# The gate matrix of a PEER layer: summed in HBM by GpSimd's indirect DMAs instead of multiplied out of one-hot matrices

## Chip, cores and metric

The kernel runs on one core of a Trainium2 chip. The metric is the device time of one execution in microseconds, here the median of three runs.

## What is computed

Two transformer-like blocks on 256 tokens of width 2048, in float32. The change touches only the PEER layer of the first block, a mixture of 16,384 one-row experts of which each token picks 8 x 16:

```python
scores = jnp.einsum('thpc,hpnc->thpn', q, sub_keys)          # 8 heads, 2 halves, 128 keys
vals, idx = lax.top_k(scores, 16)
cand = (vals[..., 0, :, None] + vals[..., 1, None, :]).reshape(T, 8, 256)
top_vals, top_c = lax.top_k(cand, 16)
experts = (i1 * 128 + i2).reshape(T, 128)                    # i1, i2: idx of the winners
gates = jax.nn.softmax(top_vals, axis=-1).reshape(T, 128)
hdn = jax.nn.gelu(jnp.einsum('ted,td->te', expert_down[experts], x))
y = jnp.einsum('te,ted->td', gates * hdn, expert_up[experts])
```

The kernel does not gather expert rows. It multiplies all 16,384 rows of `expert_down` and of `expert_up`, and weights the hidden values of each token by a gate matrix G[expert, token] that is zero where an expert was not picked and holds the sum of its gates where it was picked (by several heads, possibly).

## The kernel before, in words

**Units.** All weights are streamed in units of 512 KB: SP loads a unit into the ring `raw` (four slots), ACT copies it rounded into `whi` (three slots), DVE writes the remainder `wlo = raw - whi`, and PE multiplies both parts with the two parts of the activations. Every engine walks through the same list of units in program order, and the work around the matmuls is hung on unit numbers: `tick(u)` on PE, `step(u)` on DVE and ACT, the loop over `now` on SP. Unit u of `whi` can be written when PE has finished unit u-3.

**Stages around the change.** `wf` is the second half of the attention's output product (units 113 to 128), `pq` the PEER query (129 to 160), `down` the product with `expert_down` (161 to 416, two units for each of 128 groups), `up` the product with `expert_up` (417 to 672). Group i of `down` gives the hidden values of experts 128 i to 128 i + 127 for all 256 tokens. ACT copies one half of the PSUM bank to `HB` (`half`), DVE adds the other (`whole`, which frees the bank), POOL multiplies by the rows' normalization (`rows3`), and ACT applies `gelu(i)`, one group later. In `up` DVE multiplies by the gates (`weight(i)`).

**Routing.** `route(k)` runs in the first 162 units of `down`, a step a unit. On DVE: top 16 of the scores (steps 0 to 39), the candidate sums (41 to 48), top 16 of those (49 to 68), the softmax (69 to 71, the exponential on ACT), the look-up of i1 and i2 (72 to 95, one operation on 1024 elements a step), for both tiles of 128 tokens. At step 96 PE transposes i1, i2 and the gates, so that a token's 128 picks lie on the partitions. Then, in steps 97 to 161, `gate_rows(n)` on DVE makes two 128x128 matrices for each of four tokens (the one-hot rows of i2; the one-hot rows of i1 times the gate), PE multiplies them (`gate_batch`: four matmuls in float32 for each of 64 batches, each token's gates as a 128x128 matrix), ACT copies the bank to `GB` and issues a store of 1 MB for every 16 tokens (`gate_out`). The scratch `g_d` in HBM then holds the gate matrix, and SP loads it in pieces of 1 MB (`load_g`) for `weight(i)` in `up`; the gates of the first two groups come to `g0` ahead of that.

Of the kernel before, what the change touches and what calls it, by code (L numbers as in the profile page):

```python
# [8 lines left out]
F32 = mybir.dt.float32  # L9
# [126 lines left out]
def _build(nc, I, out, ctx):  # L136
# [3 lines left out]
    def alloc(stack, name, shape, dt=F32):  # L140
# [40 lines left out]
    g_d = nc.dram_tensor("gate_scratch", (16, 128, 2048), F32, kind="Internal").ap()  # L181
    g_v = g_d.rearrange("b p (m n c) -> m p b n c", m=16, c=16)
# [36 lines left out]
    g0 = alloc(E_, "g0", [128, 16, 2, 16])  # L219
    rows3 = alloc(E_, "rows3", [128, 256])  # L220

# [16 lines left out]
    GT = hb(25088, 256).rearrange("p (t h n) -> p t h n", t=2, h=8)  # L238
    GS = hb(25344, 32).rearrange("p (s t h) -> p s t h", s=2, t=2)
    JT = hb(25856, 768).rearrange("p (s c) -> p s c", s=3)  # L240
    AB = hb(26624, 2048).rearrange("p (i s c n) -> p i s c n", i=2, s=2, c=4)
    GB = hb(28672, 4096).rearrange("p (i n c) -> p i n c", i=2, c=16)
# [76 lines left out]
    JTF = [plan.side() for _ in range(2)]  # L319
    GBF = [plan.side() for _ in range(64)]  # L320
# [39 lines left out]
    ROUTE = 162  # L360
# [45 lines left out]
    def _(e):  # L406
# [9 lines left out]
        def load_g(n, a=0, z=8):  # L416
            i = n % 2
            if n >= 2:
                w.wait_ge(s_um, 8 * n - 8)
            e.dma_start(gbuf[:, i, :].rearrange("p (b n c) -> p b n c", b=16, c=16)[:, :, a:z, :].bitcast(F32),  # L420
                        g_v[n][:, :, a:z, :]).then_inc(s_gl[i], 16)
# [10 lines left out]
        for u in range(NRAW, NU + NRAW + NSPL):  # L432
# [21 lines left out]
            if now == G["down", 120].end:  # L454
                w.wait_ge(s_gw[0], 128)
                w.wait_ge(s_gw[1], 128)
                e.dma_start(g0[:, :, :, :], g_v[0][:, :, 0:2, :]).then_inc(s_g0, 16)
# [39 lines left out]
    def _(e):  # L497
# [88 lines left out]
        def route(k):  # L586
            if k == 96:
                w.wait_ge(s_rc, 40)
                b, b2 = vacant(JTF[0]), vacant(JTF[1])
                for t in range(2):  # L590
                    turn_round(b[:, t * 128:t * 128 + 128], IX[:, 0, t, :])
                for t in range(2):
                    turn_round(b[:, 256 + t * 128:384 + t * 128], IX[:, 1, t, :])
                for t in range(2):
                    tr = turn_round(b2[:, t * 128:t * 128 + 128], GT[:, t, :, :].rearrange("p h n -> p (h n)"))
                tr.then_inc(s_jt, 1)
            if 98 <= k <= 161:
                gate_batch(k - 98)

# [49 lines left out]
        def tick(u):  # L649
# [12 lines left out]
            if DOWN0 <= u < DOWN0 + ROUTE:  # L662
                route(u - DOWN0)
# [193 lines left out]
    def _(e):  # L857
# [131 lines left out]
        def top16(p, lists, val, idx, base):  # L989
            n = len(val)  # L990
            o = 8 * (p // 3)
            for i in lists:
                src, v, ix = val[i]
                before = base + p * n + i + 1 - n
                if p:
                    w.wait_ge(s_top, before)
                if p in (0, 3):
                    e.max(v[:, o:o + 8], src).then_inc(s_top, 1)
                if p in (1, 4):
                    e.max_index(ix[:, o:o + 8], v[:, o:o + 8], src).then_inc(s_top, 1)  # L1000
                if p == 2:
                    e.match_replace(src, v[:, 0:8], src, -3.0e38).then_inc(s_top, 1)

        one = [(SC[:, t, 2 * h + s, :], V16[:, t, h, s, :], I16[:, t, h, s, :]) for t in range(2) for h in range(8) for s in range(2)]
        two = [(CD[:, t, h, :], TV[:, t, h, :], TC[:, t, h, :]) for t in range(2) for h in range(8)]

        def gate_rows(n):
            i = n % 2
            for fill in JTF:
                evacuated(fill)  # L1010
            if n >= 2:
                w.wait_ge(s_gb, n - 1)
            for c in range(4):
                t = n * 4 + c
                e.tensor_scalar(AB[:, i, 0, c, :], iota, JT[:, 0, t:t + 1], None, ALU.is_equal).then_inc(s_oh, 1)  # L1015
                e.tensor_scalar(AB[:, i, 1, c, :], iota, JT[:, 1, t:t + 1], JT[:, 2, t:t + 1], ALU.is_equal, ALU.mult).then_inc(s_oh, 1)  # L1016

        def route(k):
            if k < 40:
                p, q = k // 8, k % 8  # L1020
                if k == 0:
                    for fill in SCF:
                        evacuated(fill)
                top16(p, range(4 * q, 4 * q + 4), one, None, 0)
            if k == 40:
                w.wait_ge(s_top, 160)
                e.tensor_copy(hb(22528, 512), hb(22016, 512, U32)).then_inc(s_rc, 1)
            if 41 <= k < 49:
                t, h0 = (k - 41) // 4, 2 * ((k - 41) % 4)
# [3 lines left out]
            if 49 <= k < 69:  # L1033
                p, q = (k - 49) // 4, (k - 49) % 4
                w.wait_ge(s_rc, 9)
                top16(p, range(4 * q, 4 * q + 4), two, None, 160)
            if k == 69:
                w.wait_ge(s_top, 240)
                e.tensor_scalar(hb(23552, 256, U32), hb(23296, 256, U32), 4, None, ALU.logical_shift_right).then_inc(s_rc, 1)
                e.tensor_scalar(hb(23808, 256, U32), hb(23296, 256, U32), 15, None, ALU.bitwise_and).then_inc(s_rc, 1)  # L1040
                w.wait_ge(s_rc, 11)
                e.tensor_copy(hb(24064, 512), hb(23552, 512, U32)).then_inc(s_rc, 1)
            if k == 70:
                tt(GT, TV, TV[:, :, :, 0:1].to_broadcast([128, 2, 8, 16]), ALU.subtract).then_inc(s_rc, 1)
            if k == 71:
                w.wait_ge(s_gx, 1)
                e.tensor_reduce(GS[:, 0], GT, AX, ALU.add).then_inc(s_rc, 1)
                w.wait_ge(s_rc, 14)
                e.reciprocal(GS[:, 1], GS[:, 0]).then_inc(s_rc, 1)
                w.wait_ge(s_rc, 15)  # L1050
                tt(GT, GT, GS[:, 1].unsqueeze(3).to_broadcast([128, 2, 8, 16]), ALU.mult).then_inc(s_rc, 1)
# [897 lines left out]
```

## Time and profile before

| | |
|---|---|
| median of three runs | 2939.56 us (2937.03 to 2940.48) |
| the profiled execution: its own time | 2936.61 us |
| its span, first to last instruction | 2934.8 us |
| busy share: PE, DVE, ACT, POOL | 98%, 65%, 48%, 4% |
| HBM traffic | 190 GB/s over the span |

PE is TensorE's matmuls, DVE is VectorE, ACT is ScalarE, POOL is GpSimd, SP is SyncE (it issues DMAs only). A busy share is an average over stages with different limits. Times in the rows are microseconds from the start of the span unless they are marked ns.

### The profile page before, as it was taken

Reading aid. Unit: us, or ns where it says so; the run is one execution under the profiler, and the core shown is the slowest. Engines: PE = TensorE matmul, PEld = TensorE weight load, DVE = VectorE, ACT = ScalarE, POOL = GpSimd, SP = SyncE. Lnnn points to the kernel's source line nnn. Section 1 sums busy time; section 2 is a strip of 40 time slices with the busy share of each in tenths; the row PEclk is TensorE's granted clock in tenths of the full one; section 3 lists DMA queues with packets and bytes.
Section 4 is the critical chain, followed back from the end, with each engine's and each line's share of the span. In section 5 each row is a group of like instructions: output and inputs, shape, how many; then the busy total and the mean of one; then the engine's idle time right before and its main releaser. Section 6 shows DMA issues by size and latency. Waiting matters only on the chain. (4 is left out here: it accounts for less than half of the span.)

```text
span 2934.8 us, 40340 instructions
## 1 busy us (share of the span) xinstructions
PE 2862.8 (98%) x15486; PEld 2465.3 (84%) x15486; DVE 1898.3 (65%) x3196; ACT 1413.9 (48%) x2024; POOL 103.9 (4%) x132
## 2 busy tenths in 40 slices
PE   8999999999999999999999999997999999999998
PEld 6878888888899988887888888886888888999886
DVE  5556665688999964455555555556677766555555
ACT  4444654444545544444444444445554545444454
POOL 0000000011211111110000000000000000000000
PEclk9999999999999999999999999998999999999999
DMA  7643456555556665567766776764554455555554
GB/s 253 209 147 119 137 177 223 161 188 190 189 195 216 215 208 188 190 193 220 222 213 216 226 230 221 240 207 132 186 172 145 147 159 193 187 187 187 183 195 152
DMA packets 180783, 558.94 MB, mean 190 GB/s; under 512 B 20704, under 2 KB 51696, under 8 KB 177648
## 3 DMA queue, kind: packets, MB, share of 16 engines
q1 hardware_dynamic: 177856, 538.48, 57.1%
q10 hardware_dynamic: 2736, 17.89, 1.5%
q8 instruction: 124, 2.03, 0.3%
q14 instruction: 67, 0.55, 0.1%
HBM read 535.31 MB, written 20.99 MB: 190 GB/s over the span
## 5 line engine op out<-in xcount | busy, mean ns | idle before, releaser
L871 DVE TENSOR_TENSOR wlo<-raw,whi 128x1024 fp32r<-128x1024 f32 (+1 forms) x965 | 1182.4, 1226 | 880.7 <-ACT whi L1507 876.4
L1507 ACT ACTIVATE whi<-raw 128x1024 fp32r<-128x1024 f32 (+1 forms) x965 | 1016.1, 1055 | 932.3 <-PE bank L501 916.2
L501 PE MATMUL bank<-aX,whi 128*128 128x512 f32 (+1 forms) x4000 | 1014.4, 395 | 2.5 <-ACT whi L1507 1.4
L501 PE MATMUL bank<-whi,aX 128*128 128x512 f32 x3008 | 933.9, 391 | 16.2 <-ACT whi L1507 12.2
L501 PEld LDWEIGHTS bank<-aX,whi 128*128 128x128 f32 (+1 forms) x4000 | 717.1, 188 | 136.7 <-issue 3.6
L501 PEld LDWEIGHTS bank<-whi,aX 128*128 128x128 f32 x3008 | 566.0, 188 | 135.6 <-ACT whi L1507 11.9
L501 PE MATMUL bank<-wlo,aX 128*128 128x512 f32 x1504 | 587.1, 390 | 2.0 <-DVE wlo L871 1.9
L501 PEld LDWEIGHTS bank<-aX,wlo 128*128 128x128 f32 (+1 forms) x3984 | 542.7, 190 | 40.1 <-DVE wlo L871 0.5
L501 PE MATMUL bank<-aX,wlo 128*128 128x256 f32 (+1 forms) x3984 | 557.7, 282 | 0.1
L501 PEld LDWEIGHTS bank<-wlo,aX 128*128 128x128 f32 x1504 | 283.1, 188 | 62.7 <-DVE wlo L871 4.4
L1507 ACT ACTIVATE aX<-HB 128x256 fp32r<-128x256 f32 x128 | 53.4, 418 | 214.6 <-DVE HB L874 214.6
L1493 POOL TENSOR_TENSOR HB<-HB,rows 128x256 f32<-128x256 f32 x128 | 103.7, 810 | 1220.5 <-DVE HB L874 1220.5
L1507 ACT ACTIVATE HB<-bank 128x256 f32<-128x256 f32 (+1 forms) x208 | 91.3, 439 | 111.3 <-PE bank L501 109.6
L1016 DVE TENSOR_SCALAR HB<-small,HB 128x128 f32<-128x128 f32 x256 | 100.3, 392 | 0.0
L874 DVE TENSOR_TENSOR aX<-HB,aX 128x256 fp32r<-128x256 f32 x128 | 54.4, 425 | 61.0 <-ACT aX L1507 61.0
L501 PE MATMUL bank<-HB 128*128 128x128 f32 x576 | 75.0, 275 | 3.1 <-DVE HB L874 3.1
L501 PEld LDWEIGHTS bank<-HB 128*128 128x128 f32 x576 | 69.8, 192 | 3.5 <-issue 3.2
L1015 DVE TENSOR_SCALAR HB<-small,HB 128x128 f32<-128x128 f32 x256 | 70.3, 275 | 0.0
L874 DVE TENSOR_TENSOR HB<-bank,HB 128x256 f32<-128x256 f32 x144 | 60.2, 418 | 0.8 <-ACT HB L1507 0.8
L1507 ACT ACTIVATE HB<-HB 128x256 f32<-128x256 f32 x129 | 53.1, 412 | 2.1 <-POOL HB L1493 1.9
L1507 ACT ACT_TABLE_LOAD x35 | 44.9, 1283 | 18.2 <-DVE dn L939 12.5
L874 DVE TENSOR_TENSOR HB<-HB,aX 128x256 f32<-128x256 f32 x126 | 52.8, 419 | 0.0
(208 smaller groups left out, 1740.9 us busy)
## 6 DMA issues: line engine op xcount, KB each, us to landing
raw<-in_w_down SPq DMA_DIRECT2D x256, 512.0 KB, 3.6
raw<-in_w_up SPq DMA_DIRECT2D x256, 512.0 KB, 3.9
raw<-in_w_in SPq DMA_DIRECT2D x176, 512.0 KB, 3.8
raw<-in_w_out SPq DMA_DIRECT2D x32, 512.0 KB, 3.5
raw<-in_w_pq SPq DMA_DIRECT2D x32, 512.0 KB, 3.6
gate_scratch<-HB ACTq DMA_DIRECT2D x16, 1024.0 KB, 4.8
raw<-in_w_o SPq DMA_DIRECT2D x32, 512.0 KB, 4.3
raw<-in_w_pg SPq DMA_DIRECT2D x32, 512.0 KB, 4.2
```

The costliest lines, as they stand in the source:

```text
L501: return e.matmul(o, lhsT, rhs, start=start, stop=stop, skip_group_check=True)
L871: e.tensor_tensor(wlo[:, s, 0:n], raw[:, r, 0:n], whi[:, s, 0:n].bitcast(F32), ALU.subtract).then_inc(s_lo, 1)
L874: return e.tensor_tensor(o, a, b, op)
L1015: e.tensor_scalar(AB[:, i, 0, c, :], iota, JT[:, 0, t:t + 1], None, ALU.is_equal).then_inc(s_oh, 1)
L1016: e.tensor_scalar(AB[:, i, 1, c, :], iota, JT[:, 1, t:t + 1], JT[:, 2, t:t + 1], ALU.is_equal, ALU.mult).then_inc(s_oh, 1)
L1493: e.tensor_tensor(h, h, rows3[:, :], ALU.mult).then_inc(s_hr3, 1)
L1507: return e.activation(o, i, f, **k)
```

## The change

The gate matrix is no longer multiplied out on PE.

- SP writes zeros over all 16 MB of `g_d` in 16 DMAs of 1 MB, one every third unit from unit 113 on; POOL fills the source with zeros first.
- Routing is done for token tile 0 in 49 steps and then for tile 1 in 49 steps. Its last step computes `place` = expert x 256 + token, the element of `g_d` to which a gate belongs.
- POOL issues 256 indirect DMAs (`scatter`), one for each tile, head and rank: 128 single elements of 4 bytes, each added to its place in HBM. Two heads of a token can pick the same expert, so the first of the 16 DMAs of a head waits until all DMAs of the head before it, of the same tile, have landed. The heads stand in the order (0,0) to (0,4), then in turn (0,5), (1,0), (0,6), (1,1), (0,7), (1,2), then (1,3) to (1,7).
- POOL multiplies by `rows3` only in groups 0 to 47, and issues three scatters behind each of groups 26 to 47; DVE does the multiplication from group 48 on. POOL issues the other scatters in one go, then loads `g0`, for which DVE waits at group 124. SP waits for all scatters at the start of `up`.
- Transposes, one-hot rows, matmuls, copies and stores of the gates are gone, and the scratch is laid out so that a gate load has pieces of 1 KB instead of 512 B.

```diff
+    g_d = nc.dram_tensor("gate_scratch", (128 * 128 * 256, 1), F32, kind="Internal").ap()
+    g_z = g_d.rearrange("(q n) o -> q (n o)", q=128)
+    g_v = g_d.rearrange("(i p t) o -> p i (t o)", p=128, t=256)
...
-    JTF = [plan.side() for _ in range(2)]
-    GBF = [plan.side() for _ in range(64)]
-    ROUTE = 162
+    ROUTE = 98
+    ZERO0 = G["wf", 0].first
+    OWN3 = 48
...
+            if ZERO0 <= now < ZERO0 + 48 and (now - ZERO0) % 3 == 0:
+                z = (now - ZERO0) // 3
+                w.wait_ge(s_zs, 1)
+                e.dma_start(g_z[:, z * 2048:z * 2048 + 2048], zeros).then_inc(s_zf, 16)
             if now == UP0:
                 w.wait_ge(s_mm, UP0)
+                for t in range(2):
+                    w.wait_ge(s_gs[t], 2048)
                 load_g(0, 2, 8)
                 load_g(1)
...
-        def gate_batch(n):
-            w.wait_ge(s_oh, 8 * n + 8)
-            b = vacant(GBF[n])
-            for c in range(4):
-                last = mm(b[:, c * 128:c * 128 + 128], AB[:, n % 2, 1, c, :], AB[:, n % 2, 0, c, :], True, True)
-            last.then_inc(s_gb, 1)
...
+        def route(step):
+            t, k = step // 49, step % 49
+            top, rc = 120 * t, 26 * t
...
+            if k == 48:
+                w.wait_ge(s_rc, rc + 24)
+                w.wait_ge(s_tok, 2)
+                e.scalar_tensor_tensor(IX[:, 0, t, :], IX[:, 0, t, :], 128.0, IX[:, 1, t, :], ALU.mult, ALU.add).then_inc(s_rc, 1)
+                w.wait_ge(s_rc, rc + 25)
+                e.tensor_scalar(place[:, t, :], IX[:, 0, t, :], 256.0, st[:, 22 + t:23 + t], ALU.mult, ALU.add).then_inc(s_rc, 1)
...
+            h = HB[:, i * 256:i * 256 + 256]
+            whole(G["down", i], h)
+            if i >= OWN3:
+                evacuated(G["down", i].fills[0])
+                tt(h, h, rows3[:, :], ALU.mult).then_inc(s_hr3v, 1)
...
+        def scatter(t, h, n):
+
+            if n == 0:
+                w.wait_ge(s_rc, 26 * t + 26)
+                w.wait_ge(s_zf, 256)
+                if h:
+                    w.wait_ge(s_gs[t], 256 * h)
+            c = 16 * h + n
+            e.indirect_dma_start(g_d, bass.IndirectOffsetOnAxis(ap=place[:, t, c:c + 1], axis=0), gate[:, t, c:c + 1], None,
+                                 compute_op=ALU.add).then_inc(s_gs[t], 16)
+
+        w.wait_ge(s_ht, 32)
+        e.memset(zeros, 0.0).then_inc(s_zs, 1)
+        order = [(0, h) for h in range(5)] + [(x % 2, 5 + x // 2 if x % 2 == 0 else x // 2) for x in range(6)] + [(1, h) for h in range(3, 8)]
+        todo = [(t, h, n) for t, h in order for n in range(16)]
+        at = 0
         w.wait_ge(s_free[R3F[0]], R3F[1])
-        for i in range(128):
+        for i in range(OWN3):
             b, n = G["down", i].fills[0]
             h = HB[:, i * 256:i * 256 + 256]
             w.wait_ge(s_free[b], n)
             e.tensor_tensor(h, h, rows3[:, :], ALU.mult).then_inc(s_hr3, 1)
+            if i >= 26:
+                for x in todo[at:at + 3]:
+                    scatter(*x)
+                at += 3
+        for x in todo[at:]:
+            scatter(*x)
+        for t in range(2):
+            w.wait_ge(s_gs[t], 2048)
+        e.dma_start(g0[:, :, :], g_v[:, 0:2, :]).then_inc(s_g0, 16)
```

On PE, where the gate matmuls begin (behind the units of step 96). The rows of the kernel before; `bank<-HB` of four matmuls is one batch, `bank<-small,HB` the transposes:

```order
L501 MATMUL bank<-aX,wlo 128x256 x8
L513 MATMUL bank<-small,HB 128x128 x6
L501 MATMUL bank<-aX,whi 128x512 x8
L501 MATMUL bank<-aX,wlo 128x256 x8
L501 MATMUL bank<-aX,whi 128x512 x8
L501 MATMUL bank<-aX,wlo 128x256 x8
L501 MATMUL bank<-HB 128x128 x4
L501 MATMUL bank<-aX,whi 128x512 x8
L501 MATMUL bank<-aX,wlo 128x256 x8
L501 MATMUL bank<-HB 128x128 x4
```

The same place in the changed kernel:

```order
L503 MATMUL bank<-aX,whi 128x512 x8
L503 MATMUL bank<-aX,wlo 128x256 x8
L503 MATMUL bank<-aX,whi 128x512 x8
L503 MATMUL bank<-aX,wlo 128x256 x8
L503 MATMUL bank<-aX,whi 128x512 x8
L503 MATMUL bank<-aX,wlo 128x256 x8
```

Nothing is left on PE between two units of `down`.

On POOL in the changed kernel, around groups 29 to 32 (`L1484` is the multiplication by `rows3`, `L1471` a scatter):

```order
L1484 TENSOR_TENSOR HB<-HB,rows 128x256 [waits s_free2]
L1471 DMA gate_scratch<-gate,place 4194304x1 x3
L1484 TENSOR_TENSOR HB<-HB,rows 128x256 [waits s_free3]
L1471 DMA gate_scratch<-gate,place 4194304x1 x3
L1484 TENSOR_TENSOR HB<-HB,rows 128x256 [waits s_free0]
L1471 DMA gate_scratch<-gate,place 4194304x1
L1471 DMA gate_scratch<-gate,place 4194304x1 [waits s_gs0]
L1471 DMA gate_scratch<-gate,place 4194304x1
L1484 TENSOR_TENSOR HB<-HB,rows 128x256 [waits s_free1]
```

Before, POOL had 128 such multiplications and nothing between them. The row with `s_gs0` is the first scatter of head 1, and a multiplication now stands behind it in POOL's queue.

On SP in the changed kernel, around the end of `wf` (`L457` writes zeros, `L446` stores the block's activations, `L453` loads the keys, `L415` loads units):

```order
L415 DMA raw<-in_w_pq 128x1024 [waits s_lo] x3
L457 DMA gate_scratch<-HB 128x2048
L415 DMA raw<-in_w_pq 128x1024 [waits s_lo]
L446 DMA h_scratch<-X 128x4096 [waits s_free3,s_free0,s_free2,s_free1]
L453 DMA HB<-in_keys 128x2048 [waits s_nt,s_free5,s_free6,s_free4,s_free7,s_spill]
L415 DMA raw<-in_w_pq 128x1024 [waits s_lo] x2
L457 DMA gate_scratch<-HB 128x2048
L415 DMA raw<-in_w_pq 128x1024 [waits s_lo] x3
```

Before, the rows of zeros were not there, and the 1 MB stores of the gates stood on ACT's queue in the middle of `down`.

## Rows read from the trace of the kernel before

**Rows 1.** The page: busy us of engines; its costliest group (count, busy us, mean ns)

```profile
PE 2862.8 (98%) x15486; PEld 2465.3 (84%) x15486; DVE 1898.3 (65%) x3196; ACT 1413.9 (48%) x2024; POOL 103.9 (4%) x132
...
L871 DVE TENSOR_TENSOR wlo<-raw,whi 128x1024 fp32r<-128x1024 f32 (+1 forms) x965 | 1182.4, 1226 | 880.7 <-ACT whi L1507 876.4
```

**Rows 2.** Waits of PE, the longest in total: us, times, longest us

```profile
PE bank L513 <- DVE scr L905: 17.4, 1, 17.4
```

**Rows 3.** Timeline of POOL: groups 47, 81, 102, 124, 127 of `down`

```profile
818.50 0.73 POOL L1493 TENSOR_TENSOR HB<-HB,rows 128x256 f32<-128x256 f32 x1 [4.84 <-DVE HB L874]
...
1066.95 0.74 POOL L1493 TENSOR_TENSOR HB<-HB,rows 128x256 f32<-128x256 f32 x1 [3.79 <-DVE HB L874]
...
1184.27 0.74 POOL L1493 TENSOR_TENSOR HB<-HB,rows 128x256 f32<-128x256 f32 x1 [4.85 <-DVE HB L874]
...
1307.18 0.85 POOL L1493 TENSOR_TENSOR HB<-HB,rows 128x256 f32<-128x256 f32 x1 [4.85 <-DVE HB L874]
...
1323.93 0.73 POOL L1493 TENSOR_TENSOR HB<-HB,rows 128x256 f32<-128x256 f32 x1 [4.84 <-DVE HB L874]
```

**Rows 4.** Instructions by line, 818 to 1062 us: count, busy us, mean ns

```profile
L1016 DVE TENSOR_SCALAR HB<-small,HB 128x128 f32<-128x128 f32 x256 | 100.3, 392 | 0.0
...
L1015 DVE TENSOR_SCALAR HB<-small,HB 128x128 f32<-128x128 f32 x256 | 70.3, 275 | 0.0
L501 PE MATMUL bank<-HB 128*128 128x128 f32 x512 | 67.6, 275 | 0.0
...
L1507 ACT ACTIVATE HB<-bank 128x512 f32<-128x512 f32 x64 | 38.4, 599 | 109.6 <-PE bank L501 109.6
```

**Rows 5.** Windows: us; busy of PE, PEld, DVE, ACT, POOL; clock, DMA share, GB/s

```profile
460.00:470.00 10.00, 10.00 (x62) 8.96 (x61) 5.57 (x7) 3.45 (x4) 0.00 (x0) 1.00 0.83 306
...
706.00:762.00 56.00, 56.00 (x323) 49.29 (x322) 53.64 (x130) 29.89 (x43) 9.36 (x10) 1.00 0.59 189
...
1067.00:1300.00 233.00, 233.00 (x1335) 204.96 (x1334) 115.50 (x125) 112.92 (x167) 30.98 (x42) 1.00 0.61 190
...
1400.00:1500.00 100.00, 100.00 (x443) 82.78 (x442) 59.12 (x74) 44.44 (x56) 0.00 (x0) 1.00 0.70 225
...
1980.00:2020.00 40.00, 40.00 (x178) 33.10 (x178) 23.39 (x29) 17.68 (x22) 0.00 (x0) 1.00 0.61 196
```

**Rows 6.** Timeline of a plain group of `down`: start, duration, engine

```profile
1072.54 0.74 POOL L1493 TENSOR_TENSOR HB<-HB,rows 128x256 f32<-128x256 f32 x1 [4.85 <-DVE HB L874]
...
1076.55 0.41 ACT L1507 ACTIVATE HB<-HB 128x256 f32<-128x256 f32 x1
...
1078.12 1.06 ACT L1507 ACTIVATE whi<-raw 128x1024 fp32r<-128x1024 f32 x1 [1.16 <-PE bank L501]
```

**Rows 7.** Timeline: POOL beside DVE, in `route` and in `gate_rows`

```profile
757.04 1.65 POOL L1493 TENSOR_TENSOR HB<-HB,rows 128x256 f32<-128x256 f32 x1 [3.91 <-DVE HB L874]
...
758.20 1.58 DVE L871 TENSOR_TENSOR wlo<-raw,whi 128x1024 fp32r<-128x1024 f32 x1
...
840.63 0.80 DVE L1016 TENSOR_SCALAR HB<-small,HB 128x128 f32<-128x128 f32 x1
...
841.54 0.33 DVE L1016 TENSOR_SCALAR HB<-small,HB 128x128 f32<-128x128 f32 x1
```

**Rows 8.** DMA queue of ACT, and DMA issues: KB each, us to landing

```profile
q10 hardware_dynamic: 2736, 17.89, 1.5%
...
gate_scratch<-HB ACTq DMA_DIRECT2D x16, 1024.0 KB, 4.8
...
g<-gate_scratch SPq DMA_DIRECT2D x1, 256.0 KB, 5.0
...
c_scratch<-cT SPq DMA_DIRECT2D x1, 16.0 KB, 2.6
```

**Rows 9.** Timeline and waits: what an issue takes, ACT behind the spill

```profile
852.11 0.33 ACTq L1581 DMA_DIRECT2D gate_scratch<-HB  x1
...
ACT HB L1507 <- DMA h_scratch<-X: 1.7, 1, 1.7
```

More of the change, by code:

```diff
@@ L987, in turn, with top16 @@
                     e.tensor_copy(dst[:, 2 * fp:2 * fp + 2, :].rearrange("p a c -> p (a c)"), banks[b]).then_inc(s_free[b], 1)
-        def top16(p, lists, val, idx, base):
-            n = len(val)
+        def top16(p, val, i, done):
+            src, v, ix = val[i]
             o = 8 * (p // 3)
[L992 to L1016, printed above, removed]
@@ L1018, in route @@
-        def route(k):
-            if k < 40:
-                p, q = k // 8, k % 8
+            if p:
+                w.wait_ge(s_top, done + (p - 1) * len(val) + i + 1)
+            if p in (0, 3):
+                e.max(v[:, o:o + 8], src).then_inc(s_top, 1)
+            if p in (1, 4):
+                e.max_index(ix[:, o:o + 8], v[:, o:o + 8], src).then_inc(s_top, 1)
+            if p == 2:
+                e.match_replace(src, v[:, 0:8], src, -3.0e38).then_inc(s_top, 1)
+        one = [[(SC[:, t, 2 * h + s, :], V16[:, t, h, s, :], I16[:, t, h, s, :]) for h in range(8) for s in range(2)] for t in range(2)]
@@ L1021, in route @@
+        two = [[(CD[:, t, h, :], TV[:, t, h, :], TC[:, t, h, :]) for h in range(8)] for t in range(2)]
+        def route(step):
+            t, k = step // 49, step % 49
+            top, rc = 120 * t, 26 * t
+            if k < 20:
                 if k == 0:
-                    for fill in SCF:
+                    for fill in SCF[4 * t:4 * t + 4]:
                         evacuated(fill)
[L1024 to L1027, printed above, removed]
@@ L1028, in route @@
-            if 41 <= k < 49:
-                t, h0 = (k - 41) // 4, 2 * ((k - 41) % 4)
+                for i in range(4 * (k % 4), 4 * (k % 4) + 4):
+                    top16(k // 4, one[t], i, top)
+            if k == 20:
+                w.wait_ge(s_top, top + 80)
+                e.tensor_copy(hb(22528 + 256 * t, 256), hb(22016 + 256 * t, 256, U32)).then_inc(s_rc, 1)
+            if 20 <= k < 24:
+                h0 = 2 * (k - 20)
                 o = CD[:, t, h0:h0 + 2, :].rearrange("p h (a b) -> p h a b", a=16)
@@ L1052, in route @@
[L1052 to L1054 removed]
+            if 24 <= k < 34:
+                w.wait_ge(s_rc, rc + 5)
+                for i in range(4 * (k % 2), 4 * (k % 2) + 4):
+                    top16((k - 24) // 2, two[t], i, top + 80)
+            if k == 34:
+                w.wait_ge(s_top, top + 120)
+                tc, tp = hb(23296 + 128 * t, 128, U32), hb(23552, 512, U32).rearrange("p (s t n) -> p s t n", s=2, t=2)
+                e.tensor_scalar(tp[:, 0, t, :], tc, 4, None, ALU.logical_shift_right).then_inc(s_rc, 1)
+                e.tensor_scalar(tp[:, 1, t, :], tc, 15, None, ALU.bitwise_and).then_inc(s_rc, 1)
+                w.wait_ge(s_rc, rc + 7)
+                e.tensor_copy(TF[:, :, t, :, :].rearrange("p s h n -> p s (h n)"), tp[:, :, t, :]).then_inc(s_rc, 1)
```

135 lines of the change are left out of this document (42 added, 93 removed).

## The prediction

> **What bounds the kernel now.** First the page's busy times: PE 98% of the span, DVE 65%, ACT 48%, POOL 4% [rows 1]. Then PE's waits: the longest is a single one of 17.4 us, at the seam behind `up` [rows 2]. So nearly every microsecond of matmuls is a microsecond of time, and what DVE, ACT, POOL or the DMAs do costs nothing as long as PE does not wait for it. Then the stage: POOL's multiplications follow DVE's `whole`, once a group, so their starts are a ruler for `down`. From group 102 (1184.27) to group 127 (1323.93) it is 25 groups in 139.66 us, 5.586 us a group, 2.793 us a unit. From group 47 (818.50) to group 81 (1066.95) it is 34 groups in 248.45 us [rows 3]. PE is busy all through `down` [rows 5], so that stretch is longer by PE's own extra work.
>
> **What it removes.** 34 plain groups are 34 x 5.586 = 189.9 us. The stretch with the transposes and the 64 gate batches takes 248.45, so 58.5 us go, 0.9 us a batch. The row of the gate matmuls says 67.6 us busy for 512 records [rows 4]. I take 58.5, because overlap with the units' matmuls is already out of it. On DVE 100.3 + 70.3 us of one-hot rows go, on ACT 38.4 us of copies [rows 4]; both lie beside PE and free nothing by themselves. The 16 stores of 1 MB on ACT's queue go too.
>
> **What it adds to DVE.** 80 multiplications by `rows3`. DVE is busy 115.5 of 233 us in the plain part, 2.8 us a group [rows 5], and a POOL operation of the same shape takes 0.74 us [rows 3], so even at that price a group has 3.5 of 5.59 us. Covered by half a group of idle DVE. Routing itself keeps its density: the same operations a step, in two runs of 49 steps instead of one of 96 for both tiles. In the densest part DVE is busy 53.64 of 56 us [rows 5] and PE does not wait there. The two new operations of a tile's last step are on 128 elements, about 0.3 us each by the one-hot rows' 275 ns [rows 4]. DVE may come behind by about half a microsecond once a tile. A remainder can be late by much more before PE notices: PE frees a slot three units ahead and needs the new contents two units (5.59 us) later, ACT's split takes 1.06 us [rows 6] and DVE's remainder 1.23 [rows 1]; so a split can be late by 4.5 us, a remainder by 3.3. Cost: nothing.
>
> **What it adds to the DMAs, first the zeros.** 16 MB, the same bytes as the gate stores that go, but now in front of weight loads on SP, in `wf` and `pq`. ACT's queue moved 17.89 MB in 1.5% of 2934.8 us, 44 us, so 2.6 us of the 16 engines for 1 MB [rows 8]. A unit takes about 0.6 of 2.793 us = 1.68 [rows 5, 3]. Three units and one zero DMA: 5.0 + 2.6 = 7.6 of 8.4 us, a share of 0.91. It fits on average. At the seam of `wf` and `pq` it does not: the share is 0.83 already there (460 to 470) [rows 5], ACT waits 1.7 us for the 2 MB spill [rows 9], and SP can load nothing until the spill has landed. One zero DMA in the same rings puts the landing off by 2.6 us, another follows two units later. A split can be late by 4.5 us, as above. From nothing to about 8 us (spill and keys each behind a whole zero DMA of 2.6, and the 1.7 that is waited for today: 6.9, and one more for what collides besides); I take 3 us.
>
> **What it adds to POOL: 256 scatters.** The trace has no indirect DMA and none that POOL issues. Let c be the time for which one holds POOL's queue. From below: a DMA issue on ACT's queue takes 0.33 us [rows 9]. From above: the smallest store to HBM takes 2.6 us from issue to landing [rows 8], and an issue should not hold the queue longer than a whole small DMA. The ends are far apart and nothing is near to either: software must compute 128 addresses, which is more than an issue and less than a round trip. I take the middle, 1.47 us. Three things hang on c.
>
> (1) Groups 26 to 47, three scatters behind each multiplication. POOL needs 3c + 0.81 a group (0.81 is POOL's 103.9 us over 128) [rows 1] and has 5.586. At 1.47 that is 5.2: it keeps up; it falls behind above c = 1.59. Queued behind is the next multiplication, for that ACT's `gelu`, behind that ACT's split, behind that PE. The slack of the chain: `gelu` starts 3.3 us after POOL's end (1073.28 to 1076.55), ACT then idles 1.16 us, and the split has 4.5 us [rows 6], together 9 us. Four times in these 22 groups a head must wait for the one before it, a landing of some 2.6 us [rows 8]. Each alone is inside the 9 us. If POOL never catches up between them, the loss is L1 = 22 (3c - 4.78) + 4 x 2.6 - 9.
>
> (2) The other 190, back to back, from 819 us on. DVE needs `g0` at group 124, which came at 1307.2 [rows 3] and comes 58.5 us earlier: at 1248.7, a budget of 429 us. Needed: 190 c, seven landings in the open (2.6 each; the alternating heads hide the rest) and the load of `g0`, 5.0 us [rows 8]. L2 = 190 c + 23 - 429. At 1.47 it is 302: done more than 120 us early. Late above c = 2.14.
>
> (3) DMA time. An element of 4 bytes is a packet. With gate loads of 512-byte pieces the share is 0.70 at 225 GB/s, without them 0.61 at 196 [rows 5]: in 100 us, 144 engine-us for 2.9 MB or 5700 packets, 25 ns each. Twice that for an add, which must also read: 8 packets an engine make 0.4 us a scatter, a share of 0.27 at c = 1.47, on top of 0.61. It fits.
>
> All three are nothing at the value taken. The Trainium skill, page "DMA: Bandwidth & Descriptors", section "Latency and other measured facts", gives about 1 us until the first byte of a DMA whose descriptors GpSimd writes, and calls it the emission overhead; by that c would be 1.0 and the sum the same. No row here shows it.
>
> **The sum.** The profiled execution: 2936.6 - 58.5 + 3 = 2881.1 us. The median of the runs stands 3.0 us above that execution, so 2884 us.
>
> **Rivals.**
>
> A. POOL is a little too slow, c from 1.6 to 2.2: PE is paced by POOL in groups 26 to 47. For it: DVE and POOL hold each other up. A multiplication that meets DVE's operation on two SBUF inputs took 1.65 us instead of 0.74, and DVE's own then took 1.58 instead of 1.23 [rows 1, 7]; a 128-element operation of DVE took 0.80 instead of 0.33 beside POOL [rows 7]. A scatter must read its places from SBUF. DVE's such operations fill 2.9 of 5.6 us a group, so a read waits 0.52 x 0.61 = 0.3 us on average: c = 1.8, L1 = 15 us, 2899 us. At c = 2.0 it is 28 us, 2912 us. The Trainium skill, page "SBUF — State Buffer", section "Who interferes with whom", says that a DVE instruction with two SBUF inputs contends with a GpSimd instruction that reads SBUF. By that rule, the trace agrees with 1.65 beside 0.74 us. Against it: the slack of 9 us, and a scatter's read is small. Chance 0.2.
>
> B. The other side, one mechanism: POOL's queue is held for more than 2.2 us a scatter, because the queue waits out most of each DMA. There L1 + L2 = 42 + 12 us eat the gain. At 2.4: 55 + 50, 2989 us; at 2.6: 68 + 88, about 3040 us. For it: the add needs a read and a write, and the smallest store lands after 2.6 us [rows 8]. Against it: issues on the other queues hold them 0.33 us for a transfer that lands after 4.8 [rows 8, 9]; an issue does not wait for a landing there. Chance 0.21.
>
> C. The DMA rings fill: an added element costs the engine 100 ns instead of 50, four times a packet of 512 bytes, as its read and its write follow each other. 0.8 us a scatter at c = 1.47 is a share of 0.54, with the weights 1.15, over 280 us: up to 42 us lost, 2884 to 2926 us. Against it: 25 ns a packet in the only stretch that tells. Chance 0.06.
>
> D. The change gives almost nothing because losses of A and C just cancel the 58 us: within 6 us of 2939.6. Chance 0.05.
>
> **The numbers.** My forecast, POOL keeps up and the zeros cost 0 to 8 us, has 0.48 and its own range is 2876 to 2895. A 0.2, B 0.21, C 0.06, D 0.05. What a measurement of this kernel can tell from no change is 0.2%, 6 us. Faster: the forecast, A and C, 0.74 less a little of A's upper end, 0.72. Same: 0.06. Slower: B and the rest, 0.22. The range must leave out no more than 2 in 10: from 2873 (the whole 58.5 us, and a seam that gets shorter) to 2965, which takes in the forecast, A, C, D and the near end of B.
>
> **What would show it.** Right: `down` at 5.59 us a group from group 48 to 127; scatters on POOL at 1 to 1.6 us; `g0` loaded near 1120 us; PE idle in `wf` and `pq` by at most a few us more. Wrong: in groups 26 to 47 ACT waits for POOL and a group takes more than 5.6 us (A); DVE waits at group 124 for `g0`, and SP behind it at the start of `up` (B); ACT's splits wait for `raw` while scatters run (C); or ACT and PE wait around 450 to 540 us for the zeros by more than 8 us.

## The result, and the profile after

The changed kernel takes **3001.34 us** (median of four runs, 2995.3 to 3003.97) against 2939.97 us (four runs, 2937.03 to 2940.48): ratio 1.0209, 95% interval 1.0196 to 1.0222. It is 61 us slower. The forecast was 2884 us, and the range ended at 2965.

From the page of the changed kernel, the rows that answer to [rows 1], and two groups of POOL (`L1471` is a scatter, `L1484` the multiplication by `rows3`; count, busy us, mean ns, idle us before them):

```profile
PE 2824.2 (94%) x14968; PEld 2420.9 (81%) x14968; DVE 1808.4 (60%) x2777; ACT 1381.6 (46%) x1963; POOL 591.5 (20%) x310
...
L1471 POOL DMA_INDIRECT gate_scratch<-gate,place x256 | 547.2, 2137 | 101.6 <-issue 76.5
...
L1484 POOL TENSOR_TENSOR HB<-HB,rows 128x256 f32<-128x256 f32 x48 | 53.2, 1107 | 319.5 <-DVE HB L853 319.5
```

Its waits (us in total, times, longest):

```profile
ACT HB L1507 <- POOL HB L1484: 92.0, 20, 7.1
...
DVE HB L853 <- DMA g<-gate_scratch: 86.2, 1, 86.2
...
PE bank L503 <- DVE wlo L850: 83.3, 5, 81.2
...
POOL gate_scratch L1471 <- DMA gate_scratch<-gate,place: 25.1, 10, 3.6
```

PE now waits 81.2 us in one piece for a `wlo` of DVE. DVE had not made it because it stood 86.2 us for the load of `g0`. And ACT waited 20 times for POOL's multiplication. Both kinds of wait were named in the prediction, as what would show it wrong.

To see where the time went I use the start of DVE's `whole` in groups 24, 52, 124, 125 and 127 of `down` as a ruler. Before:

```profile
689.51 0.42 DVE L874 TENSOR_TENSOR HB<-bank,HB 128x256 f32<-128x256 f32 x1
...
854.85 0.42 DVE L874 TENSOR_TENSOR HB<-bank,HB 128x256 f32<-128x256 f32 x1
...
1306.68 0.42 DVE L874 TENSOR_TENSOR HB<-bank,HB 128x256 f32<-128x256 f32 x1
...
1323.43 0.42 DVE L874 TENSOR_TENSOR HB<-bank,HB 128x256 f32<-128x256 f32 x1
```

After (here group 125 too, the second row from the end):

```profile
692.37 0.42 DVE L853 TENSOR_TENSOR HB<-bank,HB 128x256 f32<-128x256 f32 x1
...
886.64 0.42 DVE L853 TENSOR_TENSOR HB<-bank,HB 128x256 f32<-128x256 f32 x1
...
1288.88 0.42 DVE L853 TENSOR_TENSOR HB<-bank,HB 128x256 f32<-128x256 f32 x1
...
1378.94 0.42 DVE L853 TENSOR_TENSOR HB<-bank,HB 128x256 f32<-128x256 f32 x1
...
1388.79 0.42 DVE L853 TENSOR_TENSOR HB<-bank,HB 128x256 f32<-128x256 f32 x1
```

| stretch | worked out | us |
|---|---|---|
| up to group 24 | 692.37 - 689.51 | +2.9 |
| groups 24 to 52, against 28 plain ones | 886.64 - 692.37 - 28 x 5.587 | +37.8 |
| groups 52 to 124, against 72 plain ones | 1288.88 - 886.64 - 72 x 5.587 | 0.0 |
| groups 124 to 127, against before | (1388.79 - 1288.88) - (1323.43 - 1306.68) | +83.2 |
| the gate matrices, gone | [rows 3] | -58.5 |

The sum is +65.4, which is 1388.79 - 1323.43. The spans differ by 67.2 (3002.0 and 2934.8). The other 1.8 come behind group 127: by a `wlo` of `up` that starts at 1423.92 instead of 1357.13 the difference is 66.8, after a stretch in which PE's granted clock fell to half once more (last section). So what was to be removed was removed, 58.5 us, and two waits gave back 121.

**How a scatter meets `wlo`.** The timeline of DVE and POOL in the changed kernel's plain part (start, duration, then what ended the idle time before it):

```profile
977.68 1.23 DVE L850 TENSOR_TENSOR wlo<-raw,whi 128x1024 fp32r<-128x1024 f32 x1 [0.78 <-ACT whi L1507]
977.84 2.49 POOL L1471 DMA_INDIRECT gate_scratch<-gate,place  x1 [0.31 <-issue]
980.47 1.22 DVE L850 TENSOR_TENSOR wlo<-raw,whi 128x1024 fp32r<-128x1024 f32 x1 [1.56 <-ACT whi L1507]
980.64 2.48 POOL L1471 DMA_INDIRECT gate_scratch<-gate,place  x1 [0.30 <-issue]
...
983.27 1.23 DVE L850 TENSOR_TENSOR wlo<-raw,whi 128x1024 fp32r<-128x1024 f32 x1 [0.77 <-ACT whi L1507]
983.43 2.49 POOL L1471 DMA_INDIRECT gate_scratch<-gate,place  x1 [0.30 <-issue]
```

A scatter starts every 2.79 us, exactly one a unit, and each 0.16 us after a `wlo` has begun. The same queue while DVE stands:

```profile
1290.70 1.55 POOL L1471 DMA_INDIRECT gate_scratch<-gate,place  x1 [0.30 <-issue]
1292.56 1.55 POOL L1471 DMA_INDIRECT gate_scratch<-gate,place  x1 [0.30 <-issue]
...
1369.41 1.55 POOL L1471 DMA_INDIRECT gate_scratch<-gate,place  x1 [0.30 <-issue]
1372.95 0.78 POOL L1493 DMA_DIRECT2D g<-gate_scratch  x1 [1.98 <-DMA gate_scratch<-gate,place]
```

Now 1.55 us and a gap of 0.30, 1.86 a scatter. And three scatters that meet DVE in other ways, in the routing:

```profile
730.50 2.11 POOL L1471 DMA_INDIRECT gate_scratch<-gate,place  x1 [0.31 <-issue]
...
745.62 0.28 DVE L977 FIND_INDEX8 HB<-HB 128x8 uint32<-128x128 f32 x1
745.75 1.56 POOL L1471 DMA_INDIRECT gate_scratch<-gate,place  x1 [1.62 <-DMA gate_scratch<-gate,place]
```

The one at 730.50 began in the middle of a `wlo` that ran from 729.96 to 731.19, and ended at 732.61, 1.42 us behind it. The one at 977.84 ended 1.42 us behind its `wlo` too (980.33 against 978.91). All 256 scatters of the changed kernel, sorted by the DVE operation in which they started:

- 182 started inside a `wlo`. 179 of them end 1.42 to 1.47 us behind that `wlo`, whenever they began; the other three began in its last 0.04 us and last 1.56 us.
- 67 started with DVE idle: 1.55 us in the middle of their number.
- 5 started in an operation with one SBUF input (`FIND_INDEX8`, `MATCH_REPLACE8`, or a `whole`, whose other input is in PSUM): four last 1.56 us, and the first scatter of the run 1.75.
- 2 started in DVE's own multiplication by `rows3`, again two SBUF inputs: they last 1.77 us and end 1.43 behind it.

I read this so: a scatter reads SBUF in its first 0.13 us (1.55 less 1.42); the read waits for the end of a DVE operation with two SBUF inputs; then come 1.42 us of its own.

From this follows the lock. Behind a delayed scatter the next one starts 1.42 + 0.30 = 1.72 us after the end of `wlo`. The next `wlo` starts 2.79 - 1.23 = 1.56 us after that end. So the next scatter begins 0.16 us inside it and is delayed again, and so on as long as DVE runs at this pace.

The Trainium skill, page "SBUF — State Buffer", section "Who interferes with whom", says that a DVE instruction with two SBUF inputs contends with a GpSimd instruction that reads SBUF, and that a DMA which seems stalled by DVE is one whose descriptors GpSimd writes. By that rule the trace agrees: 2.49 us in `wlo`, 1.56 in operations with one input.

### The profile page after: what moved, and what is told of

It is laid out like the page before. It is cut to its first block and busy times, and to the rows that moved or that the text cites. A ratio compares the mean times of both kernels' runs of the same rounds, so it can differ in the third digit from the quotient of the medians.

```text
span 3002.0 us, 38891 instructions
## 1 busy us (share of the span) xinstructions
PE 2824.2 (94%) x14968; PEld 2420.9 (81%) x14968; DVE 1808.4 (60%) x2777; ACT 1381.6 (46%) x1963; POOL 591.5 (20%) x310
## 5 line engine op out<-in xcount | busy, mean ns | idle before, releaser
L503 PE MATMUL bank<-aX,wlo 128*128 128x256 f32 (+1 forms) x3984 | 561.1, 283 | 81.3 <-DVE wlo L850 81.2
L1471 POOL DMA_INDIRECT gate_scratch<-gate,place x256 | 547.2, 2137 | 101.6 <-issue 76.5
L1484 POOL TENSOR_TENSOR HB<-HB,rows 128x256 f32<-128x256 f32 x48 | 53.2, 1107 | 319.5 <-DVE HB L853 319.5
L1507 ACT ACTIVATE HB<-bank 128x256 f32<-128x256 f32 x144 | 52.8, 366 | 3.5 <-DMA h_scratch<-X 3.5
L853 DVE TENSOR_TENSOR HB<-HB,g 128x256 f32<-128x256 f32 x2 | 0.8, 422 | 86.2 <-DMA g<-gate_scratch 86.2
L503 PE MATMUL bank<-wlo,mH 128*128 128x512 f32 x128 | 50.8, 397 | 0.2 <-DVE wlo L850 0.2
```

Source lines behind the costliest of these rows:

```text
L503: return e.matmul(o, lhsT, rhs, start=start, stop=stop, skip_group_check=True)
L853: return e.tensor_tensor(o, a, b, op)
L1471: e.indirect_dma_start(g_d, bass.IndirectOffsetOnAxis(ap=place[:, t, c:c + 1], axis=0), gate[:, t, c:c + 1], None, compute_op=ALU.add).the ...
L1484: e.tensor_tensor(h, h, rows3[:, :], ALU.mult).then_inc(s_hr3, 1)
L1507: return e.activation(o, i, f, **k)
```

## The experiments

Two readings stood against each other. **The lock** (theory): the second input of `wlo` holds the scatter's read, and the queue runs in step with DVE; free of it a scatter costs 1.86 us. **The scatter's own work** (rival): the queue is held by the addresses, the elements or the add, and DVE's part is a small one. A time without a range is that of a single run; the kernel before had 2940.78 beside the first four of the runs below, 2939.76 (median of seven) beside the next three and 2940.52 (of 15) beside the last three.

**Only token tile 0 is scattered** (128 of 256 scatters; the gates of tokens 128 to 255 are left out, and with them the two waits for tile 1).

```diff
-        todo = [(t, h, n) for t, h in order for n in range(16)]
+        todo = [(0, h, n) for h in range(8) for n in range(16)]
```

> The changed kernel with only the 128 scatters of token tile 0; the gates of tile 1 are left out (their places in HBM stay zero), all else is as it was, so 66 scatters stand between POOL's multiplications and 62 behind them. Both theories of why a scatter is slow agree that the wait for g0 at group 124 goes away and that the loss in groups 26 to 47 stays. Expected: 2936.6 + 2.9 (seam) + 37.8 (groups 26 to 52) - 58.5 = 2919 us; the three parts of the loss add up if it lies within 5 us of that. If the scatters also slowed DMAs or the stage behind, it would be above 2930.

Measured: 2918.61 us. The wait for `g0` is gone, and groups 24 to 52 still lose 37.1 us (whole at 692.24 and 885.80). So the two losses of the prediction are apart: L1, ACT's wait for POOL, hangs on the three scatters a group; L2, DVE's wait for `g0`, on the length of the queue. 2918.6 is 83 us below the changed kernel, the +83.2 of the table.

**A plain write instead of an add** (the gates of an expert that several heads of a token picked are no longer summed: the last one stays).

```diff
-            e.indirect_dma_start(..., gate[:, t, c:c + 1], None, compute_op=ALU.add)
+            e.indirect_dma_start(..., gate[:, t, c:c + 1], None)
```

> The changed kernel with the 256 scatters as plain writes (no add; a gate overwrites what another head put there). Theory L (a scatter holds POOL for 1.86 us, and its read of SBUF waits until DVE's operation on two SBUF inputs has ended, which locks it to one a unit of 2.79 us): nothing changes, 3001 us within 10, scatters of 2.49 us in the plain part. Rival W (the add makes a scatter slow, for GpSimd or for the DMA rings): scatters of 1.6 to 2 us in the plain part, the wait at group 124 shrinks or goes, 2920 to 2960 us.

Measured: 2883.45 us, which neither had expected. Its timeline of POOL:

```profile
974.61 0.96 POOL L1471 DMA_INDIRECT gate_scratch<-gate,place  x1 [0.30 <-issue]
975.87 1.22 POOL L1471 DMA_INDIRECT gate_scratch<-gate,place  x1 [0.30 <-issue]
977.39 0.96 POOL L1471 DMA_INDIRECT gate_scratch<-gate,place  x1 [0.30 <-issue]
```

A free scatter takes 0.96 us without the add: the add costs 0.6 us of POOL's queue, which neither reading had. And the lock is still there in another form: behind a delayed one the next comes 0.83 + 0.30 = 1.13 us after the end of `wlo`, which is before the next `wlo` (1.56), so two fit into each unit of 2.79 us, one delayed (1.22) and one not. The add alone decides which of the two forms it takes. This run could not tell the two readings apart, since it takes away 0.6 us of own work and the lock with it.

**`rows3` on DVE from group 26 on** instead of 48.

```diff
-    OWN3 = 48
+    OWN3 = 26
```

> DVE takes over the multiplications from group 26 instead of 48, so all 256 scatters stand behind each other on POOL from 704 us on. Theory L: ACT never waits for POOL (the 37.8 us of groups 26 to 52 go), but the scatters get through at 2.2 us each in the routing part and one a unit behind it, some 144 in the plain part, and 55 are left at group 124, at 1.86 us each: PE waits some 115 us there instead of 83. Sum 2936.6 + 2.9 - 58.5 + 115 = 2996 us, hardly less than 3001. Rival C (each takes 2.44 us whatever DVE does): done at 1354, a wait of 107 us, 2988 us. If the wait at 124 stayed 83 us: 2964 us.

Measured: 2971.74 us. Groups 24 to 52 take 156.42 us, 28 plain ones to 0.02 (691.03 to 847.45): L1 is gone, and DVE takes the 22 more multiplications for nothing. The wait for `g0` is 96.6 us, 10 more than before, because group 124 comes 39 us earlier (1249.69 against 1288.88) and the queue not as much. I had expected 115: 47 scatters were left at group 124 and not 55.

**`wlo` in four operations of 256 elements** in the groups beside the scatters; same DMAs, same elements, same bytes.

```diff
-                e.tensor_tensor(wlo[:, s, 0:n], raw[:, r, 0:n], ...).then_inc(s_lo, 1)
+                m = n // 4 if DOWN0 + 52 <= u < UP0 else n
+                for c in range(0, n, m):
+                    low = e.tensor_tensor(wlo[:, s, c:c + m], raw[:, r, c:c + m], ...)
+                low.then_inc(s_lo, 1)
```

> DVE's remainder (wlo) of 1024 elements in four operations of 256 from unit 52 of down to its end; same work, same DMAs, same scatters. Theory L: POOL's read waits for one operation of 0.4 us at most instead of 1.2, the lock to one a unit breaks, scatters take 1.6 to 2.0 us in the plain part, all are done before group 124, no wait for g0: 2911 to 2920 us, with the loss of groups 26 to 52 left. Rivals (the DMA rings under the weight loads, or the add, or a port that DVE keeps between operations that follow each other): scatters of 2.49 us as before, 3001 us or more.

Measured: 2907.15 us. POOL in its plain part:

```profile
983.94 1.55 POOL L1474 DMA_INDIRECT gate_scratch<-gate,place  x1 [0.30 <-issue]
985.80 1.55 POOL L1474 DMA_INDIRECT gate_scratch<-gate,place  x1 [0.30 <-issue]
987.66 1.55 POOL L1474 DMA_INDIRECT gate_scratch<-gate,place  x1 [0.30 <-issue]
```

1.86 us a scatter beside a busy DVE, and `g0` is issued at 1248.10 instead of 1372.95, before it is wanted. Nothing of the scatter's work was changed, only how long DVE holds the read at a time, and 94 us are gone. That decides for the lock. What is left against the forecast is L1: groups 24 to 52 still lose 25.2 us (693.16 to 874.78), ACT waits 81.3 us for POOL.

The release is not complete where DVE is dense. In the routing part five scatters of this run waited out two or three further pieces, 2.41 to 2.79 us each:

```profile
729.26 1.40 DVE L852 TENSOR_TENSOR wlo<-raw,whi 128x256 fp32r<-128x256 f32 x4
729.30 2.79 POOL L1474 DMA_INDIRECT gate_scratch<-gate,place  x1 [0.30 <-issue]
```

So the rival that the expectation names last, DVE keeping the port between operations that follow each other, holds at times, here for `wlo` after `wlo`; behind routing it was not seen in this run. What decides between the two is open.

**Both edits**, four pieces and `OWN3 = 26`.

> Both cures together: wlo in four operations of 256 from unit 52, and DVE multiplies by rows3 from group 26 on. Theory L, from the two single runs: no wait of ACT for POOL in groups 26 to 47 (the 27 to 38 us go, as in the run with own26), scatters at 1.86 us in the plain part (as in the run with split4). Scatters 704 us + 57 until 830 + 199 x 1.9 + landings: done near 1240, group 124 comes near 1250, so g0 (5 us) is just in time: wait 0 to 5 us. 2936.6 + 2.9 - 58.5 = 2881, range 2879 to 2890 us. If the two cures share one mechanism (ACT's wait for POOL was only a sign of the slow scatters), no more than split4 alone: 2907 us. If DVE cannot carry route, split and rows3 at once in units 52 to 98: above 2890 with PE waiting for wlo there.

Measured: 2882.81 us (median of four, 2879.78 to 2883.68), ratio to before 0.9802, 0.9786 to 0.9819.

**Two pieces of 512** and `OWN3 = 26` (the line is shown against the run before).

```diff
-                m = n // 4 if DOWN0 + 52 <= u < UP0 else n
+                m = n // 2 if DOWN0 + 52 <= u < UP0 else n
```

> The same with wlo in two operations of 512. Theory L: a scatter's read waits for the rest of one operation of 0.7 us instead of 1.2 us, so a scatter that meets one takes up to 2.1 us instead of 2.49, and whether the lock to one a unit breaks depends on 1.86 + the wait against 2.79: 2.4 us at most, so it breaks. Scatters at 2.1 on average, done near 1300: a wait of some 50 us for g0, 2930 us; with full release 2881. If only operations of 0.4 us let POOL in, 2970 as in own26.

Measured: 2877.99 us. Two pieces are enough: it came out as with full release (2881), not at the 2930 of half a release. Of this kernel, in the run below, POOL beside DVE:

```profile
980.68 1.55 POOL L1474 DMA_INDIRECT gate_scratch<-gate,place  x1 [0.30 <-issue]
981.05 1.29 DVE L852 TENSOR_TENSOR wlo<-raw,whi 128x512 fp32r<-128x512 f32 x2 [1.50 <-ACT whi L1510]
...
984.39 1.58 POOL L1474 DMA_INDIRECT gate_scratch<-gate,place  x1 [0.30 <-issue]
```

Here a scatter that begins inside a piece waits for that piece alone; the one at 984.39 is delayed by 0.03 us. (Two in the routing part waited out both pieces, 2.42 and 2.47 us.) Three scatters at 1.86 us are 5.58 us, two units are 5.59: they keep their places between the operations.

**64 tokens a scatter** (half of the tokens get no gates).

```diff
-            e.indirect_dma_start(g_d, ...(ap=place[:, t, c:c + 1], axis=0), gate[:, t, c:c + 1], ...
+            e.indirect_dma_start(g_d, ...(ap=place[0:64, t, c:c + 1], axis=0), gate[0:64, t, c:c + 1], ...
```

> The changed kernel with 64 elements a scatter instead of 128 (tokens 64 to 127 of each tile are left out); as many scatters. If the 1.56 us of a free scatter are per element (two descriptors and more for each), it takes about 0.8 to 1.0 us, two fit in a unit, no wait for g0, little loss in groups 26 to 47: 2881 to 2890 us. If they are a fixed cost: 2.49 us locked as before, 3001 us.

Measured: 2907.71 us; the wait for `g0` is gone, and groups 24 to 52 still lose 26.9 (691.81 to 875.15). Neither side of the expectation had this. A free scatter takes 1.41 us with 64 elements and 1.55 with 128, so 64 elements are 0.14 us, about a tenth of the hold. If the first 64 cost the same, some 1.27 us are a price for each DMA; that is an estimate from two points. And 0.14 us less were again enough to leave the lock. DVE and POOL there:

```profile
974.51 1.28 DVE L850 TENSOR_TENSOR wlo<-raw,whi 128x1024 fp32r<-128x1024 f32 x1 [1.56 <-ACT whi L1507]
974.53 1.41 POOL L1471 DMA_INDIRECT gate_scratch<-gate,place  x1 [0.31 <-issue]
```

Behind a delayed scatter the next one now starts 1.28 + 0.30 = 1.58 us after the end of `wlo`, 0.02 us behind the start of the next, and that is early enough: it takes 1.41 us, and `wlo` 1.28 instead of 1.23. Whoever reads first holds the other up. So three scatters fit into two units (1.41, 1.62, 1.65). Over all runs with `wlo` in one piece, scatters that began up to 0.037 us inside a `wlo` went through at once, and the earliest that was held in full began 0.038 inside (in own26). So to leave the lock a scatter need only come within 0.04 us of the start of `wlo`; in the changed kernel it came 0.16 behind.

**The best version again**, two pieces and `OWN3 = 26`, for an interval.

> The kernel of split2_own26 again, with rounds, to give it an interval. The single look had 2878 us. If the lock between scatter and wlo is the whole cause, two pieces of wlo with the late rows3 of DVE from group 26 on give 2876 to 2882 us, which is the kernel before less the 58.5 us of gate matrices, plus or minus the seam; if the look was a lucky one, the time goes to the 2883 of the version with four pieces or above.

Measured: **2880.35 us** (five runs, 2878.88 to 2882.46), ratio 0.9799, interval 0.9786 to 0.9812. It is 2.0% faster than the kernel before and 121 us faster than the change as it was made. Its groups 24 to 52 take 156.42 us (691.76 to 848.18), its `g0` is issued at 1235.1, and no wait of PE or ACT for POOL is left.

**Zeros begun later**, at the last group of `pq`, else as the best version.

```diff
-    ZERO0 = G["wf", 0].first
+    ZERO0 = G["pq", 3].first
```

> split2_own26 with the writes of zeros begun at the last group of the query product (some 50 units later), so that they no longer share SP's queue and the DMA engines with the loads at the seam. Theory (the seam's 2.9 us are the zeros' writes delaying loads of raw while only a few units are ahead): 0 to 3 us below best_split2. Rival (the loads in down have no more slack than those at the seam, so the same bytes cost the same wherever they are moved): equal to best_split2 within 1 us, or above it when the last zeros land after POOL is ready for its first scatter.

Measured: 2880.23 us (four runs, 2879.71 to 2880.76), the same. ACT's waits for `raw` of `pq` fall from 14.2 to 2.0 us, and nothing is gained. The first `whole` of `pq` comes at 456.11 instead of 458.18, but eight groups on they stand at 500.63 and 500.85. The delay at the start of `pq` is made up within `pq`.

**The kernel before with `wlo` in two pieces**, in the plain part of `down` alone.

```diff
-                e.tensor_tensor(wlo[:, s, 0:n], raw[:, r, 0:n], ...).then_inc(s_lo, 1)
+                m = n // 2 if DOWN0 + 162 <= u < UP0 else n
+                for c in range(0, n, m):
+                    low = e.tensor_tensor(wlo[:, s, c:c + m], raw[:, r, c:c + m], ...)
+                low.then_inc(s_lo, 1)
```

> The kernel before with wlo made in two operations of 512 elements in units 162 and up of down, which is where its own gate matrices end and no scatter runs. Control for the edit itself. Theory (the halves help only by giving a scatter's read its turn sooner): 2939 to 2941 us, no change from the kernel before, since PE is the bound there and DVE has a third of its time free. Rival (shorter pieces of wlo help PE by themselves): 2 us or more below the kernel before.

Measured: 2939.31 us (ten runs), ratio 0.9998, interval 0.9989 to 1.0007. The pieces themselves give nothing: two take 1.29 us instead of 1.23, and PE is the bound.

It also settled the +2.9 us up to group 24. Windows (us; busy of PE, PEld, DVE, ACT, POOL; granted clock, DMA share, GB/s) of 535 to 545, where `pq` ends: the kernel before, then before with two pieces, then the changed kernel, then split2_own26.

```profile
535.00:545.00 10.00, 6.93 (x57) 6.59 (x56) 6.00 (x8) 1.67 (x3) 0.00 (x0) 1.00 0.47 155
```

```profile
535.00:545.00 10.00, 6.93 (x41) 6.52 (x40) 4.39 (x6) 1.98 (x3) 0.00 (x0) 0.83 0.49 158
```

```profile
535.00:545.00 10.00, 6.93 (x40) 6.42 (x39) 4.48 (x7) 2.39 (x3) 0.00 (x0) 0.85 0.77 292
```

```profile
535.00:545.00 10.00, 6.93 (x58) 6.59 (x57) 6.08 (x8) 1.59 (x3) 0.00 (x0) 1.00 0.68 255
```

PE waits 3.1 us there in all four. Behind that wait the clock stayed at 1.00 in two of the profiles and was granted at 0.83 to 0.85 in the two others. The first group of `down` (its `whole`) comes at 555.43 in the kernel before and at 555.35 in split2_own26, which writes the zeros and had the clock at 1.00 too; it comes at 557.33 in the control, which has no zeros, and at 558.29 in the changed kernel. So the clock behind this wait is worth some 2 us and differs from run to run. The 0.9 us by which the changed kernel stands behind the control are within what equal code gives: own26, with zeros and a clock of 0.83, has 556.94. No cost of the zeros is shown.

## Why the prediction was wrong

**What bounds it, and the removal: right.** 34 groups of the stretch cost 5.587 us each once the gate batches were gone; best_split2's span is 57.7 us below that of the control.

**DVE's additions: right.** 80 multiplications, and in the best version 102 and most of the `wlo` of `down` in halves, cost nothing.

**The zeros: 3 us taken, 2.9 seen, and that was luck.** It was the clock behind PE's wait at the end of `pq`, which the kernel before can lose as well. ACT did wait 14.3 us for `raw` and 3.5 for the spill, and a share of 1.01 stands in the window from 470 to 500; but the units ahead of PE filled again: 2.07 us late at the start of `pq` were 0.22 eight groups on (best_split2 against best_late).

**The DMA time, against rival C: right.** In the page of best_split2 the queue of the scatters (packets, MB, share of 16 engines' span):

```profile
q0 software_dynamic: 36944, 0.41, 3.3%
```

That is 0.37 us a scatter, where 0.4 was worked out, and some 144 packets each, so with the add an element is a packet, as taken. Without the add it is not: plain_write has 8272 packets on that queue, some 32 a scatter, and 0.2%, 0.02 us a scatter. The share of all DMAs says the same of the add, and a little more of the plain write: against 0.64 in a stretch of tile0_only without scatters (1070 to 1270) it is 0.82 from 870 to 1240 in best_split2 (181 scatters, 0.37 us each) and 0.71 from 870 to 1120 in plain_write (167 scatters, 0.10 us each). So the plain element was priced too high (0.2 us for 128) and the factor of two for the add too low; that the two cancel is luck. No split of ACT waited for these transfers in `down`.

**The failed step: c, the time for which a scatter holds POOL's queue.** I took 1.47 us, the middle between a bare issue and a store's round trip. Free of DVE it is 1.86: 1.55 and a gap of 0.30. That alone would have been past the 1.59 of (1). Beside DVE's `wlo` it is 2.79, past the 2.14 of (2). The two formulas held. At 1.86 throughout, (1) gives 19 us and (2) nothing, 2903 us in all: close to the 2907 of split4. With what the trace of the changed kernel shows:

- L1: in groups 26 to 47 a scatter took 1.90 us in the mean, with 0.30 to the next, and 0.93 from the end of one to the start of the next where a multiplication stands between. A group is 5.70 + 0.60 + 0.93 = 7.23 us, so L1 = 22 (7.23 - 5.59) + 10.4 - 9 = 37.5 us; measured 37.8.
- L2: the other 190 took 2.22 + 0.30 = 2.52 us in the mean (2.79 in the lock, 1.86 for the 42 or so that ran while DVE stood). 190 x 2.52 + 23 - 429 = 73 us, and 9 more because POOL came into this part late by the slack that L1 takes off: 82; measured 83.2.

The multiplication itself is no part of the error, though its record is longer than the 0.74 of [rows 3]:

```profile
708.88 1.75 POOL L1471 DMA_INDIRECT gate_scratch<-gate,place  x1 [0.30 <-issue]
710.09 1.31 POOL L1484 TENSOR_TENSOR HB<-HB,rows 128x256 f32<-128x256 f32 x1
711.57 2.38 POOL L1471 DMA_INDIRECT gate_scratch<-gate,place  x1 [0.17 <-issue]
```

The record of the multiplication begins 0.54 us before that of the scatter ends (710.63), and ends 0.77 behind it (711.40). All 21 that follow a scatter begin 0.54 to 0.57 before its end; 18 end 0.76 to 0.77 behind it, the other three 1.18 to 1.19. Nearly everything of the error is in c.

**The rivals.** The time is that of rival B, L1 and L2 together. B's reason is refuted: the queue does not wait out the transfer, since the same DMAs ran at 1.86 us when `wlo` was cut up. The mechanism is that of rival A, which I had read from [rows 7] and then priced at 0.3 us: the share of time that DVE's two-input operations fill, times half of one. That average holds for arrivals at random. These are not: a scatter's end is set by the end of `wlo`, and so is the next one's start. In the lock the wait is 0.93 us, each time. What an operation costs beside a periodic one is to be worked out as a schedule: where does the next one start after a delayed one, and does it meet the same again?

**The bound that I didn't take.** The range held both ends of c, 0.33 and 2.6, in its chances (B at 0.21) but not in its upper limit. The measured hold of 2.79 lay above the upper end: "not longer than a whole small DMA" is no bound for a queue that waits for a port first.

The Trainium skill, page "DMA: Bandwidth & Descriptors", section "Latency and other measured facts", has about 1 us until the first byte for a DMA that GpSimd writes the descriptors of. A time to the first byte is not the time for which a queue is held, and no run here measured the first. For a plain indirect write the hold is near to that figure (0.96 us); with the add it is 1.55, which that figure would have missed.

**Open.** Why the add takes 0.6 us more of POOL isn't shown, only that it does. The number of packets alone does not give it: tokens64 has 64 fewer a scatter (80 instead of 144) and saves 0.14 us, plain_write 112 fewer and saves 0.59. That it is a read of SBUF which waits in a scatter's first 0.13 us is inferred from its times, no record shows it. And why a few scatters wait out several pieces of `wlo` is open.

## What to carry to other kernels

Work put on GpSimd's queue beside a VectorE that streams two-input operations runs in step with that stream: work out where the next one starts behind a delayed one, and don't take an average of the overlap. When the two lock, a small cut of either (two halves of `wlo`, 0.14 us less of a scatter) gives back much more than itself; here four pieces of `wlo` gave back 94 us, and two did as much beside `OWN3 = 26`, at 0.06 us a unit. And before an effect of 2 to 3 us at a seam (where one product gives way to the next) is put down to a change, look at the granted clock of that stretch in a second run of the unchanged code.

## What the runs showed of the hardware

- An indirect DMA of 128 single elements held POOL's queue 1.55 us with an add and 0.96 without, 1.41 with 64 elements and an add, with 0.30 us to the next one.
- Begun inside a DVE operation with two SBUF inputs, it ended 1.42 to 1.47 us behind that operation (1.42 + 0.13 = 1.55, its free length). Operations with one SBUF input did not delay it (1.56 us).
- In the lock its start is 0.16 us inside `wlo`; begun up to 0.04 us inside, it went through at once and `wlo` took 1.28 us instead of 1.23.
- With `wlo` in pieces it waited for its own piece, but in the routing part five of split4 and two of best_split2 waited out further ones (2.41 to 2.79 us).
- DMA time of 128 such elements: 0.37 us of 16 engines with the add (some 144 packets), 0.02 without by their own queue (some 32 packets) and 0.10 by the share of all DMAs.
- After PE had stood 81 us its clock rose, fell once more and rose again. Windows of the changed kernel behind the stand:

```profile
1376.00:1382.00 6.00, 4.05 (x14) 3.61 (x15) 5.64 (x8) 1.63 (x3) 0.00 (x0) 0.53 0.48 154
1382.00:1388.00 6.00, 4.39 (x27) 3.74 (x25) 3.51 (x7) 3.19 (x6) 0.00 (x0) 1.00 0.73 246
1389.00:1395.00 6.00, 5.65 (x13) 4.46 (x14) 0.63 (x2) 2.00 (x4) 0.00 (x0) 0.50 0.85 266
1396.00:1402.00 6.00, 6.00 (x29) 4.93 (x28) 3.21 (x4) 2.37 (x3) 0.00 (x0) 1.00 0.64 167
```

At 1.00 (2.4 GHz) from 1382 to 1388 PE was busy 4.39 of 6 us. From 1389 to 1395 it was busy 5.65 us, but at 0.50 (1.2 GHz), and got through 13 records where the last window has 29. Of the 1.8 us by which the spans differ more than the ruler at group 127, 1.4 are there by 1424; the rest was not followed.
